# Three reorderings in a one-core decoder layer kernel: a down block's high part, a product unit's high part, and the squares of the residual blocks

## What is computed

```python
x = x + concat(rmsnorm(stick_breaking(q, k, v)), rmsnorm(s5(u))) @ w_out   # q, k, v, u from rmsnorm(x) @ w_in
x = x + mem_attend(rmsnorm(x), mk, mv, w_mq, w_mo)                        # cross attention, 256 memory tokens
h = rmsnorm(x)
f = (gelu(causal_conv3(h @ w_gate)) * (h @ w_up)) @ w_down                 # w_gate, w_up: 1024 x 2816
y = rmsnorm(x + f)
```

## Time and profile before

| | before |
|---|---|
| median of three runs | 864.0 us |
| lowest, highest | 860.53, 864.13 us |
| profiled execution | 862.45 us |
| its span, first to last instruction | 860.6 us |
| granted TensorE clock, mean | 0.995 of full |
| TensorE busy | 819.7 us, 95% |
| VectorE busy | 529.0 us, 61% |
| ScalarE busy | 382.8 us, 44% |
| GpSimd busy | 202.3 us, 24% |

### The profile page before, as it was taken

One profiled execution on the slowest core, in us unless ns is written; L12 is line 12 of the kernel. 1 busy time (PEld: TensorE's weight loads), 2 busy tenths in 40 slices (PEclk: granted clock), 3 DMA queues, 4 the chain that ended last, 5 costly groups with the idle time before them and its releaser, 6 DMA issues.

```text
span 860.6 us, 17207 instructions
## 1 busy us (share of the span) xinstructions
PE 819.7 (95%) x7342; PEld 775.4 (90%) x7342; DVE 529.0 (61%) x828; ACT 382.8 (44%) x589; POOL 202.3 (24%) x157
## 2 busy tenths in 40 slices
PE   5999999998999998998999899999999999899996
PEld 4989999887979998994599899999999999899995
DVE  5969998898347635112325987888888868210013
ACT  6535414667645324122424754555545557322221
POOL 4100001110550251430025130202020224845430
PEclk9999999999999999999999999999999999999998
DMA  9211212625554394318412323222232342433302
GB/s 332 68 57 50 75 50 99 203 78 179 187 166 136 120 399 162 98 50 341 197 37 87 98 75 99 98 99 99 99 99 99 98 128 70 148 98 98 105 1 100
DMA packets 31294, 104.99 MB, mean 122 GB/s; under 512 B 3930, under 2 KB 7002, under 8 KB 28786
## 3 DMA queue, kind: packets, MB, share of 16 engines
q1 hardware_dynamic: 31218, 103.90, 35.7%
HBM read 96.28 MB, written 6.71 MB: 120 GB/s over the span
## 4 chain that ended last, share of the span: by engine, by line
PE 75%; DVE 10%; ACT 5%; DMA 4%; issue 2%; SPq 1%; POOL 1%; DVEq 0%; ACTq 0%
PE pj L696 14%; PE pj L698 14%; PE pj L697 14%; DMA w_raw<-in 4%; PE aux L703 3%; PE aux L705 3%; PE aux L704 3%; PE pj L703 3%; PE pj L705 3%; PE pj L704 3%; PE pj L1314 2%; PE aux L1245 2%; DVE h_lo L1913 1%; PE aux L778 1%; PE pj L1022 1%
## 5 line engine op out<-in xcount | busy, mean ns | idle before, releaser
L660 POOL TENSOR_TENSOR w_lo<-w_raw,w_hi 128x512 fp32r<-128x512 f32 x106 | 147.5, 1413 | 495.7 <-ACT w_hi L1458 495.6
L696 PE MATMUL pj<-h_hi,w_hi 128*128 128x260 f32 x720 | 207.2, 288 | 14.5 <-POOL w_lo L660 12.6
L698 PE MATMUL pj<-h_hi,w_lo 128*128 128x260 f32 x720 | 204.0, 283 | 0.0
L697 PE MATMUL pj<-h_lo,w_hi 128*128 128x260 f32 x672 | 190.0, 283 | 0.0
L1458 ACT ACTIVATE w_hi<-w_raw 128x1024 fp32r<-128x1024 f32 x78 | 82.5, 1057 | 183.4 <-PE pj L698 146.2
L696 PEld LDWEIGHTS pj<-h_hi,w_hi 128*128 128x128 f32 x720 | 136.2, 189 | 16.7 <-POOL w_lo L660 12.9
L698 PEld LDWEIGHTS pj<-h_hi,w_lo 128*128 128x128 f32 x720 | 136.1, 189 | 0.0
L697 PEld LDWEIGHTS pj<-h_lo,w_hi 128*128 128x128 f32 x672 | 127.0, 189 | 0.3
L660 POOL TENSOR_TENSOR wx_lo<-w_raw,wx_hi 128x512 fp32r<-128x512 f32 x36 | 48.3, 1365 | 105.2 <-ACT wx_hi L1458 105.2
L2587 DVE TENSOR_TENSOR conv<-pj,rinv 128x520 f32<-128x520 f32 x7 | 4.9, 700 | 83.3 <-PE pj L698 83.3
L696 PE MATMUL pj<-h_hi,wx_hi 128*128 128x260 f32 x176 | 50.0, 284 | 0.8 <-DVE h_lo L1913 0.8
(11 more groups left out here) (484 smaller groups left out, 2343.1 us busy)
## 6 DMA issues: line engine op xcount, KB each, us to landing
w_raw<-in SPq DMA_DIRECT2D x126, 512.0 KB, 3.7
caches<-in SPq DMA_DIRECT2D x14, 1024.0 KB, 12.4
vpg<-in SPq DMA_DIRECT2D x16, 256.0 KB, 3.0
kpg<-in SPq DMA_DIRECT2D x12, 256.0 KB, 3.0
x<-in SPq DMA_DIRECT2D x4, 520.0 KB, 7.8
out<-x SPq DMA_DIRECT2D x16, 130.0 KB, 1.9
out<-kT SPq DMA_DIRECT2D x1, 1040.0 KB
far<-in SPq DMA_DIRECT2D x1, 1024.0 KB, 4.7
```

Source lines behind the costliest of these rows:

```text
L660: nc.gpsimd.tensor_tensor(lo[:, part], w_raw[:, raw_of(n) % 4, part], hi[:, part].bitcast(F32), ALU.subtract).then_inc(lo_done, 1)
L696: pe.matmul(out, s_hi, m_hi_, start=first, stop=False)
L697: pe.matmul(out, s_hi, m_lo_, start=False, stop=False)
L698: ins = pe.matmul(out, s_lo, m_hi_, start=False, stop=last)
```

## The change

Nothing is added or taken out: every instruction is there as before, and five pieces of the programs change places.

- ScalarE, seven products: for the second and third tile of each run, unit 3's high part (`high_seven(t, 3)`) moves from behind the tap of the tile before to behind the first copy of its own tile. VectorE: its low part moves from behind the taps of the tile before to behind `read_first` of its own tile. For the first tile of each run both stay.
- ScalarE, down blocks: `high(N_DOWN + 1)` comes ahead of the first four `high_a` instead of behind them; the tap of the last tile comes behind six of them instead of four; `high(N_DOWN + 2)` comes behind that tap instead of behind the sixteenth. The gelu of the last tile comes behind ten instead of eight.
- VectorE, `residual`: `add_square` of the last tile comes ahead of `low(base + 9)` instead of behind it, in both residual stages.

```diff
--- before.py
+++ after.py
@@ -1849,6 +1849,7 @@
                 for t in run:
                     copy_chain(t, 0)
                     if t > run[0]:
+                        high_seven(t, 3)
                         ff_open(t - 1)
                     if t < run[-1]:
                         high_seven(t + 1, 0)
@@ -1860,7 +1861,6 @@
                         high_seven(t + 1, 1)
                         high_seven(t + 1, 2)
                         last_tap(t)
-                        high_seven(t + 1, 3)
                     else:
                         high(UNIT[t + 1] + 1)
                 if run[-1] + 2 in SEVEN:
@@ -1869,13 +1869,13 @@
             high(N_DOWN)
             ff_open(FT - 2)
             act.wait_ge(block_done, UNIT[FT - 1])
-            high_a(0, 4)
             high(N_DOWN + 1)
+            high_a(0, 6)
             last_tap(FT - 1)
-            high_a(4, 8)
+            high(N_DOWN + 2)
+            high_a(6, 10)
             ff_open(FT - 1)
-            high_a(8, 16)
-            high(N_DOWN + 2)
+            high_a(10, 16)
             act.wait_ge(block_done, N_DOWN)
             high_a(16, FT)
             nc.scalar.preload_act_table_set("natural_log_exp_and_others")
@@ -2359,8 +2359,9 @@
                         low(base + s + 2)
                     if s == 7:
                         split_low(7, gain, at_ + 8)
+                    add_square(j0 + s, s == 0, T, group)
+                    if s == 7:
                         low(base + s + 2)
-                    add_square(j0 + s, s == 0, T, group)
                     if base == N_MO and s in (5, 6):
                         low_form(s - 5)
                     if base == N_MO and s in (4, 5):
@@ -2557,6 +2558,8 @@
                 low_seven(run[0], 3)
                 for t in run:
                     read_first(t)
+                    if t > run[0]:
+                        low_seven(t, 3)
                     if t < run[-1]:
                         low_seven(t + 1, 0)
                     if t > run[0]:
@@ -2572,7 +2575,6 @@
                     if t < run[-1]:
                         low_seven(t + 1, 2)
                         first_taps(t)
-                        low_seven(t + 1, 3)
             first_taps(FT - 2)
             multiply(FT - 2)
             low_a(0, 4)
```

## The result

The changed kernel takes 854.4 us (median of 6 runs, 853.6 to 855.4) where the kernel before takes 863.2 (its three runs and three more, beside the changed kernel). The ratio is 0.990, with an interval of 0.988 to 0.993: faster by about 8.3 us. One of the six runs of the kernel before took 1150.2 us, far from all others; without it their median is 862.5. The prediction said 856.4, in a range of 853.0 to 861.0. The time lies in the range and the side is right; how the saving is made up is not quite as forecast, and that is what the experiments are about.

A forecast was written before the change was run, and what follows sets the result against it. TensorE, busy for 95% of the span, was taken to bound the kernel, so only its idle time could be won. Savings of 0.80 + 1.87 + 2.1 + 2.0 = 6.8 us from 863.2 gave 856.4 us, range 853.0 to 861.0.

The forecast's parts named there:

- Part 1: Both residual stages: last squares ahead of the low part let TensorE go on earlier, saving 0.80 and 1.87 us.
- Part 2: Seven-product tiles: fourth unit's high part behind the first copy saves 0.52 us in each of four runs, 2.1 us.
- Rival C: Seven-product tiles: moving the fourth high part gives nothing, VectorE's 0.2 us margin being absent; saved 4.7, 858.5 us; chance 0.08.
- Part 3: Third down block: earlier high part removes a 2.66 us hole, a new 0.63 us `a_lo` stall appears; net 2.0 us.
- Rival B: Third down block: GpSimd stands back as long as before, leaving a 2.1 us hole; saved 5.3, 857.9 us; chance 0.10.
- The fourth block: Fourth down block: GpSimd stands back until VectorE's subtractions end; its half is done at 736.05, needed at 736.8.
- Rival A: Fourth down block: GpSimd let in between VectorE's last subtractions, two end 1.2 us late; saved 5.6, 857.6 us; chance 0.12.
- Rival E: Seven-product tiles: later low part frees the raw block late, loads limit nine tiles by 0.86 us; 866.2 us; chance 0.03.
- Rival D: Whole kernel: most of the saving lost in a later wait or in scatter; about 861 us; chance 0.07.
- The sum: Whole kernel: savings of 0.80, 1.87, 2.1 and 2.0 add to 6.8 us, giving 856.4 us.

The follow-up runs named there:

- paced changed kernel: The changed kernel, with each of VectorE's last low parts of the products waiting for the one before it: 860.33 us, ratio 0.997 to the kernel before.
- sevens alone: The kernel before, with only the fourth unit's high and low part moved behind the first copy and read: 862.42 us, ratio 0.999.
- down alone: The kernel before, with only the reordering of high parts at the down blocks: 859.09 us, ratio 0.996.
- no squares: The changed kernel, with the last squares put back behind the low part in both residual stages: 859.45 us, ratio 0.997 to the kernel before.
- paced before: The kernel before, with each of VectorE's last low parts of the products waiting for the one before it: 863.58 us, ratio 1.002.
- squares alone: The kernel before, with only the last addition of squares put ahead of the low part in both residual stages: 859.33 us, ratio 0.996.
- no down: The changed kernel, with the old order of high parts at the down blocks: 857.50 us, ratio 0.996 to the kernel before.

## Why the prediction was right, and where it was not

**Part 1, 2.67 us: right.** 0.88 + 1.96 = 2.84 by the table, in both profiles of the changed kernel and alone; 2.2 and 1.6 us in the full-clock parts of two pairs of kernels, which scatter by some tenths. The addition of 1.77 us is 0.69 with nothing beside it, and TensorE goes on behind the sums when the low part is done, both as worked out.

**Part 2, 2.1 us: this is the step that failed.** It gave 0.25 us by the table and 0.2 in the full-clock part of the kernel that has it alone. The working stopped at the first copy ("with the copy first it starts at 668.76 and TensorE at 669.27. Saved 0.52 each"). The next thing that TensorE takes from ScalarE is the second copy 3 us later. In the kernel before that copy started at 672.08 and the matmul behind it at 672.74, with no wait, so none stood in the list to warn of it; but it followed a high part and a gelu that wait for VectorE, and so it did not come earlier. At 0.51 us from a copy's start to its matmul (667.17 to 667.68) it had 0.15 us to spare, less than the 0.52 to be won. The other 0.37 come back as a wait, and the matmul behind the one that waited starts 0.20 us after it instead of 0.12: 0.45 in all. That was to be read in ScalarE's rows behind the earlier trace rows, which the prediction did not follow. Rival C's result (nothing from part 2) came true, but not by its cause: VectorE's margin of 0.2 us was there, at 0.21. The kernel with the second copy first, where the 0.52 each stay, shows this. The sign that the prediction named for part 2, four waits for `sq` of 0.1 to 0.2 in place of 0.6, is in the list, and misleads: they are four new waits at the second copies.

**Part 3, 2.0 us: right, and its two terms too.** The hole of 2.66 is gone, the stall for `a_lo` was given as 0.63 and is 0.72 in the table (0.42 recorded, which with the overlap of 0.16 is 0.58; the matmul that waited holds the next for another 0.1). Net 2.1. The steps between hold as well: the halves were given for 721.5, which less the lead of 4.97 is 716.53, and start at 716.54; the product that waits was to start at 724.53 + 0.63 = 725.16, less the lead 720.19, and starts at 720.15. Rival B did not happen: no half waited there for a row of subtractions. One reading was wrong without harm: the half of 1.73 us that the prediction sets against the 5.69 is the one at 715.48, two halves earlier, not the next one.

**The fourth block: right in kind.** GpSimd stood back again: its half at 727.88 took 3.13 us, to 731.01, and VectorE's six subtractions took 3.74 undisturbed. Rival A, GpSimd let in between them, did not happen. Its price of 1.2 us counted one half; in the paced changed kernel, which forces it, four of the six last subtractions met one, and it pays 3.5 us in the full-clock part. A part of that is the price of the waits themselves.

**Rival E, slower by late loads: nothing of it.** No wait of a high part for `w_raw` shows in the tiles of seven products; the third tiles do not lose, they gain 0.25 in all. **Rival D**: the lead of the squares passes the cache loads unchanged where the clock stays up (3.19 at 388, 3.54 at 404 in the second profile of the changed kernel).

**The sum.** Right were 2.8 + 2.1 of 6.8; with the 0.25 it is 5.2 us by the table, and the full-clock part fell by 4.8 (854.4 to 849.6, over all runs). The rest of the measured 8.3 is the clock part, which fell as well, by 3.2 (6.6 to 3.4 us). The prediction had no term for it. So that the time came within 2 us of the forecast was in part luck: 1.8 us too much for part 2 were more than made up by some 3 us that were not thought of. That the holes and the stretches belong together rests on their places in the profiles, and on this: kernels with the squares' holes have clock parts of 5.7 to 7.2 us (before in three sets of runs, sevens alone, down alone, no squares, paced before); those without them and without a long hole at the down blocks have 3.1 to 4.0; with the down hole alone it is 5.3 (squares alone) and 4.1 (no down), and with new gaps at the last products 5.6 (paced, changed). What decides in which execution a hole is followed by one was not found, and the parts are means over 6 to 12 executions of each kernel; that the granted clock falls at short holes in a part of the executions is shown, a rule for when is not.

The Trainium skill, "SBUF — State Buffer", on the shared port pair, lets whoever issues first hold it for one instruction. This case agrees for single collisions (1.79 us for a subtraction of 0.69) and where halves and subtractions take turns (four subtractions in 5.04 us). It does not agree at the last row of subtractions: the half waited through several of them, 5.69 us in the kernel before and 3.13 in the changed one, and took 1.83 in the first, 3.36 for two halves in the second, once gaps were there. The Trainium skill, "TensorE: Matmul & The Clock Gate", on the HAM clock gate, says that the rate halves when TensorE has been idle. The stretches at a mean of 0.57 to 0.64 at the holes agree in kind; the same holes at 1.00 in the kernel before show that a hole of this length is not always followed by one.

## What to carry to other kernels

A copy that is brought forward helps only as far as the next thing that the same two engines exchange: follow the producer's queue to its next hand-over and read how late that one is, even if no wait for it is in the list. A short hole of TensorE, where it bounds the kernel, can cost more than its length, since in a part of the executions a stretch at half clock follows; count it at its length plus that chance (here about 3 us in the mean for about 5 us of holes that went away). And compare kernels that issue the same matmuls number by number: one profile against another held differences of 1 to 4 us ahead of the first place that the change touches.

## What was not expected of the hardware

- Holes of 0.8 to 2.7 us are, in some executions, followed by a few us at half clock, for 1.5 to 2.8 us of lost time; the same hole in another execution is not.
- GpSimd was kept out by a VectorE row without gaps until the row ended (5.69 us for a half), and a single semaphore wait between the instructions of that row let it in each time. Another row without gaps let it in of itself, so the gaps are not all that decides.
- With the waits the row takes 8.31 us instead of 3.74, of which a part is the waits' own (0.80 us per subtraction instead of 0.61, with GpSimd idle). What looks like a starved GpSimd was the cheaper of the two for TensorE.
